# Router logits from un-normed sums beside the output projection of a two-block transformer on one Trainium2 core

## The reference

```python
x = x + gate1 * (merged @ w_out)
h2 = rmsnorm(x, norm2_w) * (1.0 + scale2) + shift2
x = x + gate2 * hierarchical_moe(h2, ...)

def hierarchical_moe(h, w_rg, b_rg, w_re, b_re, w_gate, w_up, w_down):
    g_logits = hf @ w_rg + b_rg               # 4 groups, take the best
    e_logits = hf @ w_re + b_re               # 4 x 8 experts, take the best two of the group
    ...
    for e in range(32):
        act = silu(hf @ w_gate[e]) * (hf @ w_up[e])
        y = y + combine[:, e:e + 1] * (act @ w_down[e])
```

## Time and profile before

| | us |
|---|---|
| median of 3 runs (1857.8 to 1860.01) | 1859.15 |
| the profiled execution | 1859.66 |
| its span, first to last instruction | 1857.8 |
| mean granted TensorE clock | 0.938 |

### The profile page before, as it was taken

One profiled execution on the slowest core, in us unless ns is written; L12 is line 12 of the kernel. 1 busy time (PEld: TensorE's weight loads), 2 busy tenths in 40 slices (PEclk: granted clock), 3 DMA queues, 4 the chain that ended last, 5 costly groups with the idle time before them and its releaser, 6 DMA issues.

```text
span 1857.8 us, 20218 instructions
## 1 busy us (share of the span) xinstructions
PE 1670.6 (90%) x8343; PEld 1247.3 (67%) x8343; DVE 804.0 (43%) x1325; ACT 541.0 (29%) x852; POOL 54.7 (3%) x75
## 2 busy tenths in 40 slices
PE   4999999999887998989899799999999896987883
PEld 3986777777676787878788577688678775433331
DVE  5545343354353666556212684436662535111113
ACT  5334354344322322212112432331353212111111
POOL 3000000000000000000000000000000000111110
PEclk8998999999998899999999799999999987998987
DMA  4322222122223455464222122211213543999994
GB/s 126 125 91 46 68 69 68 62 71 73 68 69 110 133 165 182 159 202 136 91 91 85 46 68 69 68 56 58 69 46 138 197 167 132 387 418 420 419 390 164
DMA packets 146256, 260.33 MB, mean 140 GB/s; under 512 B 16036, under 2 KB 120640, under 8 KB 132464
## 3 DMA queue, kind: packets, MB, share of 16 engines
q1 hardware_dynamic: 140240, 249.82, 38.0%
q0 software_dynamic: 5920, 9.16, 1.4%
HBM read 253.71 MB, written 14.68 MB: 144 GB/s over the span
## 4 chain that ended last, share of the span: by engine, by line
PE 44%; DVE 4%; issue 2%; DMA 1%; ACT 1%; POOLq 0%; DVEq 0%; ACTq 0%
PE psum L2206 8%; PE psum L2207 8%; PE psum L2208 8%; PE psum L2768 7%; PE psum L2785 3%; PE psum L2746 1%; PE psum L2395 1%; PE psum L2597 1%; DVE WL L1413 0%; PE psum L2415 0%; PE psum L2343 0%; PE psum L2353 0%; PE psum L2352 0%; DMA Xg<-h_rows,tok 0%; PE psum L2374 0%
## 5 line engine op out<-in xcount | busy, mean ns | idle before, releaser
L2206 PE MATMUL psum<-AH,WH 128*128 128x512 f32 (+1 forms) x1240 | 497.9, 402 | 46.5 <-DVE WL L1413 15.0
L2207 PE MATMUL psum<-AL,WH 128*128 128x512 f32 (+1 forms) x1240 | 481.6, 388 | 0.0
L2208 PE MATMUL psum<-AH,WL 128*128 128x512 f32 (+1 forms) x1240 | 478.4, 386 | 0.0
L2206 PEld LDWEIGHTS psum<-AH,WH 128*128 128x128 f32 x1240 | 240.4, 194 | 110.8 <-DVE WL L1413 26.5
L1413 DVE TENSOR_TENSOR WL<-raw,WH 128x2048 fp32r<-128x2048 f32 (+1 forms) x100 | 226.6, 2267 | 201.0 <-ACT WH L913 201.0
L2208 PEld LDWEIGHTS psum<-AH,WL 128*128 128x128 f32 x1240 | 240.5, 194 | 48.0
L2207 PEld LDWEIGHTS psum<-AL,WH 128*128 128x128 f32 x1240 | 240.9, 194 | 45.7 <-issue 3.1
L913 ACT ACTIVATE WH<-raw 128x2048 fp32r<-128x2048 f32 (+1 forms) x100 | 189.0, 1890 | 196.0 <-PE psum L2208 129.3
L2768 PE MATMUL psum<-WE,XT 128*64 128x512 f32 x544 | 133.3, 646 | 25.4 <-issue 24.5
L2768 PEld LDWEIGHTS psum<-WE,XT 128*64 128x64 f32 x544 | 48.4, 149 | 108.7 <-issue 108.7
L1820 DVE SCALAR_TENSOR_TENSOR cst<-araw,pcol,cst 128x256 f32<-128x256 f32 x168 | 81.6, 486 | 6.0
(11 more groups left out here) (481 smaller groups left out, 1896.3 us busy)
## 6 DMA issues: line engine op xcount, KB each, us to landing
raw<-w_in SPq DMA_DIRECT2D x45, 1024.0 KB, 5.2
WE<-w_gate SPq DMA_DIRECT2D x34, 1024.0 KB, 20.8
WE<-w_up SPq DMA_DIRECT2D x34, 1024.0 KB, 29.0
WE<-w_down SPq DMA_DIRECT2D x34, 1024.0 KB, 28.6
araw<-w_ada SPq DMA_DIRECT2D x24, 1024.0 KB, 5.2
raw<-w_ffn_in SPq DMA_DIRECT2D x22, 1024.0 KB, 5.2
raw<-w_ffn_out SPq DMA_DIRECT2D x11, 1024.0 KB, 4.9
raw<-w_out SPq DMA_DIRECT2D x8, 1024.0 KB, 5.1
```

The source lines that it names most:

```text
L2206: MM(dst, lh, rh, start=first, stop=False)
L2207: MM(dst, lh, rl, start=False, stop=False)
L2208: return MM(dst, ll, rh, start=False, stop=last)
```

## The change

The logits are taken from the raw `hT`. With gain = (1 + scale2) * norm2_w, the normed token is rms * x * gain + shift2, so its logit is rms * (x @ (gain * wr)) + (shift2 @ wr + bias). Accordingly:

- `router_shift` (PE, 8 products of 36 columns) and `router_scale` (DVE) put shift2 @ wr into `rb` and scale `wr` by gain. PE does this right after group 0 of `wo2`, where it now waits for `wr`.
- `rows_of(c)` is run by PE for each chunk c, seven times between dense products and once behind the last: 4 sums of squares, 4 logit products (tokens on the partitions, 36 columns) and 4 transposes of `hT`. ACT copies each set of transposes to `xtm`.
- Behind the last slab the spread of the norm, `H2`, its 32 transposes, `lgT` and the later transposes of `hT` are gone. DVE multiplies the logits by rms and adds `rb`.
- `h2t` is now `xtm` times rms, 1024 columns by ACT from SBUF, in a ring of two rows of tokens; POOL stores it, not SP, and its gather waits for all four stores.
- gain and shift2 are applied at the experts' copies `XT`: four instructions of 128 columns on ACT and four on DVE for a tile, where one of 512 stood on each. Their columns in the experts' order come by a small round trip through DRAM (`gs_dram`), started at `km` 0.
- `ranks` makes 5 products (128, 128, 96, 64 and 32 columns) where 14 stood.
- The constants of the routing (`routing_numbers`) are computed by DVE at the start of `wo2`.
- The second half of tile 1 moves to a slot over `AH`, and is loaded after the last dense product; so are both halves of tile 2.

```diff
 (SP, expert loads)
                 if s["name"] == ("wo2", 2):
                     sp.wait_ge(*when("m2_lo", KC))
                     load_expert(sp, 0, 1, NE // 2)
+                if s["name"] == ("wo2", 3):
                     load_expert(sp, 1, 0, 1)
-                if s["name"] == ("wo2", 3):
-                    load_expert(sp, 1, 1, NE // 2 + 1)
...
             sp.wait_ge(*when("dense_ready", len(GROUPS)))
+            load_expert(sp, 1, 1, NE // 2 + 1)
             load_expert(sp, 2, 0, 2)
-
-            for t in range(NB):
-                sp.wait_ge(*when("h2t_copied", 2 * t + 2))
-                sp.dma_start(h2_dram[P * t:P * t + P, :], h2t[:, t, :]).then_inc(S_("h2_stored"), 16)
-            sp.wait_ge(*when("spots_used", 1))
+            sp.wait_ge(*when("n_two_summed", KC))
+            load_expert(sp, 2, 1, NE // 2 + 2)
             sp.wait_ge(*when("overflow_ready", 1))
-            load_expert(sp, 2, 1, NE // 2 + 2)
 (POOL)
-            pool.wait_ge(*when("h2_stored", 16 * NB))
+            for t in range(NB):
+                pool.wait_ge(*when("h2t_copied", t + 1))
+                pool.dma_start(h2_dram[P * t:P * t + P, :], h2t[:, t % 2, :]).then_inc(S_(f"h2_stored{t % 2}"), 16)
+            for n in range(2):
+                pool.wait_ge(*when(f"h2_stored{n}", 16 * len(range(n, NB, 2))))
             pool.wait_ge(*when("tokens_ready", 1))
 (ACT)
+            def rows_copy(c):
+                act.wait_ge(*when("x_major", c + 1))
+                nc.scalar.activation(xtm[:, :, P * c:P * c + P], bank(6 + c % 2).rearrange("p (t n) -> p t n", t=NB), ACT.Copy
+                                     ).then_inc(S_("xtm_copied"), 1)
...
-                nc.scalar.activation(XT[:, t % 2, 0:512], bank(0), ACT.Copy).then_inc(S_("xt_even"), 1)
+                for k in range(4):
+                    nc.scalar.activation(XT[:, t % 2, P * k:P * k + P], bank(0, P, P * k), ACT.Identity, scale=gain8[:, k:k + 1],
+                                         bias=shift8[:, k:k + 1]).then_inc(S_("xt_even"), 1)
 (DVE)
+            def router_scale():
+                dve.wait_ge(*when("router_shift", 1))
+                link(V.tensor_tensor(rb, bank(7, NG + NE), rb, ALU.add))
+                dve.wait_ge(*when("router_landed", 32))
+                V.tensor_tensor(wr, wr, gain.unsqueeze(2).to_broadcast([P, KC, NG + NE]), ALU.mult).then_inc(S_("router_scaled"), 1)
...
-            norm_apply("n_two", hT, gain, False, out_name="h2_ready", shift=shift2, dst=H2)
...
-            dve.wait_ge(*when("logits_ready", 1))
+            dve.wait_ge(*when("router_mm", 1))
             link(V.tensor_tensor(lg, bank(5, NB * (NG + NE)).rearrange("p (t n) -> p t n", t=NB),
-                                 rb.unsqueeze(1).to_broadcast([P, NB, NG + NE]), ALU.add))
+                                 stat[:, 48:52].unsqueeze(2).to_broadcast([P, NB, NG + NE]), ALU.mult))
+            link(V.tensor_tensor(lg, lg, rb.unsqueeze(1).to_broadcast([P, NB, NG + NE]), ALU.add))
 (PE)
+            def router_shift():
+                pe.wait_ge(*when("router_landed", 32))
+                for c in range(KC):
+                    ins = MM(bank(7, NG + NE), shift2[:, c:c + 1].to_broadcast([P, P]), wr[:, c, :], start=c == 0, stop=c == KC - 1)
+                ins.then_inc(S_("router_shift"), 1)
+
+            def rows_of(c):
+                if c == 0:
+                    pe.wait_ge(*when("router_scaled", 1))
+                pe.wait_ge(*when("n_two_squared", c + 1))
+                for t in range(NB):
+                    ins = MM(bank(4, 1, t), sq2[:, c % 4, P * t:P * t + P], ones[:, 0:1], start=c == t == 0, stop=c == KC - 1,
+                             skip_group_check=True)
+                ins.then_inc(S_("n_two_summed"), 1)
+                for t in range(NB):
+                    ins = MM(bank(5, NG + NE, (NG + NE) * t), hT[:, c, P * t:P * t + P], wr[:, c, :], start=c == t == 0,
+                             stop=c == KC - 1, skip_group_check=True)
+                if c == KC - 1:
+                    ins.then_inc(S_("router_mm"), 1)
+                if c >= 2:
+                    pe.wait_ge(*when("xtm_copied", c - 1))
+                for t in range(NB):
+                    ins = nc.tensor.transpose(bank(6 + c % 2, P, P * t), hT[:, c, P * t:P * t + P], ident)
+                ins.then_inc(S_("x_major"), 1)
...
-                for t in range(NB):
-                    for b in range(t + 1):
-                        MM(bank(7, NE, NE * t), K("strict") if b == t else ones, both[:, b, :], start=b == 0, stop=b == t)
-                for b in range(NB):
-                    ins = MM(bank(7, NE, NE * NB), ones, both[:, b, :], start=b == 0, stop=b == NB - 1)
+                MM(bank(7, NB * NE), K("strict"), both.rearrange("p t n -> p (t n)"), start=True, stop=False, skip_group_check=True)
+                for b in range(1, NB + 1):
+                    n = NE * (NB + 1 - b)
+                    ins = MM(bank(7, n, NE * b), ones, both.rearrange("p t n -> p (t n)")[:, 0:n], start=False, stop=b == NB,
+                             skip_group_check=True)
...
-                    for _ in pieces(s):
-                        pass
+                    for j, _ in enumerate(pieces(s)):
+                        if s["name"][0] == "wo2":
+                            i = s["name"][1]
+                            if (i, j) == (0, 1):
+                                router_shift()
+                            if (i, j) == (1, 0):
+                                rows_of(0)
+                            if i and j == 1:
+                                rows_of(2 * i - 1)
+                            if i and j == 2:
+                                rows_of(2 * i)
                     end(s)
-            norm_pe("n_two")
+            rows_of(KC - 1)
```

More of the change, by code:

```diff
@@ L1825, in _, with routing_numbers @@
             summed = []
+            def routing_numbers():
+                link(V.tensor_scalar(later, K("expert"), -1000.0, None, ALU.add))
+                link(V.tensor_tensor_scan(iota, ones, ones, -1.0, ALU.mult, ALU.add))
+                link(V.tensor_scalar(thr[:, 0, :], iota[:, 1:8], float(CAP), 0.5, ALU.mult, ALU.add))
+                link(V.tensor_scalar(thr[:, 1, :], thr[:, 0, :], -1.0, None, ALU.add))
+                link(V.tensor_scalar(places[:, 0, :], K("expert"), NE // 2 - 0.5, float(CAP), ALU.is_ge, ALU.mult))
+                link(V.scalar_tensor_tensor(places[:, 1, :], places[:, 0, :], -0.5 * NE / CAP, K("expert"), ALU.mult, ALU.add))
+                for c in range(2):
+                    V.tensor_scalar(ids[:, NB * c:NB * c + NB, 0], K("token"), 1.0, None, ALU.add).then_inc(S_("dve_chain"), 1)
+                    V.tensor_scalar(ids[:, NB * c:NB * c + NB, 1], K("token"), 2.0, c + 1.0, ALU.mult, ALU.add).then_inc(S_("dve_chain"), 1)
+                    chain.n += 2
+            def router_scale():
[3 more added lines that the diff above has]
+                V.tensor_tensor(wr, wr, gain.unsqueeze(2).to_broadcast([P, KC, NG + NE]), ALU.mult).then_inc(S_("router_scaled"), 1)
             def modulation():
@@ L2158, in xt_copy @@
                 dve.wait_ge(*when("tx_done", t + 1))
-                V.tensor_copy(XT[:, t % 2, 512:], bank(1)).then_inc(S_("xt_odd"), 1)
+                for k in range(4, KC):
+                    V.tensor_scalar(XT[:, t % 2, P * k:P * k + P], bank(1, P, P * (k - 4)), gain8[:, k:k + 1], shift8[:, k:k + 1],
+                                    ALU.mult, ALU.add).then_inc(S_("xt_odd"), 1)
             def gated(t):
@@ L2329, in ml_guard @@
             def ml_guard(h):
[L2330 to L2331 removed]
+                pe.wait_ge(*(when("ml_h", h) if h else when("gs_rows", 1)))
                 sel = ident[0:4, h:h + 1].to_broadcast([4, P])
@@ L2618, in end @@
                     columns_of_pending()
-                if k in ("wo", "wo2") and name[1]:
-                    norm_sums("n_ffn" if k == "wo" else "n_two", 2 * name[1] - 2, 2 * name[1])
+                if k == "wo" and name[1]:
+                    norm_sums(2 * name[1] - 2, 2 * name[1])
                 if name == ("qm", 0):
                     gates_rows()
+                if name == ("km", 0):
+                    pe.wait_ge(*when("gain_two", 1))
+                    for n, x in enumerate((gain, shift2)):
+                        ins = nc.tensor.transpose(bank(7, P, P * n)[0:KC], x, ident)
+                    ins.then_inc(S_("gs_turned"), 1)
                 if name == ("qm", 1):
```

184 lines of the change are left out of this document (84 added, 100 removed).

## The result

| | us |
|---|---|
| before, median of 4 runs (1857.8 to 1860.01) | 1859.24 |
| after, median of 4 runs (1876.13 to 1877.57) | 1877.14 |
| after, span of the profiled execution | 1874.3 |

The changed kernel is slower: the ratio is 1.0096, with a 95% interval of 1.0083 to 1.0108. The forecast was 1863.2 with a range up to 1872.0, so the direction was right, the time lies 13.9 us above the forecast and 5.1 us outside the range.

The account below looks back on a forecast made before the run. Experts are bound by weight loads, so the end follows tile 0's gate_up, behind a PE-bound dense stretch and a chain. Dense stretch +23.9 us, chain -19.9, total +4.0: forecast 1863.2 us, range 1855.5 to 1872.

Parts of the forecast that it names:

- (a): Dense wo2 stretch: seven rows_of calls of 2.29 us each, less two blocks of sums removed; net +12.4 us.
- (b): Dense wo2 stretch: the eight products of router_shift add 1.7 us.
- (e): At km 0: two transposes and their copy for the small DRAM round trip add 0.3 us.
- (c): Behind group 0 of wo2: PE stands waiting for wr, +5.4 us; lower bound 2.5.
- (d): Behind the wait for wr: PE's clock falls to half, slowing small and dense products, +4.1 us; lower bound 1.7.
- first rival: wr lands before PE asks, so (c) and (d) vanish: -9.5 us, 1853.7 us, faster; chance 0.12.
- (f): Chain behind the last group's addition: logits lg done 4.8 us after it instead of 19.3, gain 14.5 us.
- (g): Chain from logits through ranks: unchanged up to both, then five rank products in 2.7 us; gain 3.0 us.
- (i): Before the gather: four token-row stores delay its issue to 28.9 us after the last group; loss 1.4, bounds 0 and 4.
- (k): Tile 0's XT copy: four operations instead of one add 0.3 us; in later tiles the loads cover the delay.
- The third: Rival: the clock falls inside the rows_of calls, 2.35 us each, seven costing 16: 1879 us; chance 0.15.
- The fourth: Rival: stores land late and the gather runs beside a load, +3 to +5 us: 1866 to 1869 us; chance 0.13.

Follow-up runs that it names:

- e5: Kernel before with only the XT copies split into four instructions of 128 columns each on ACT and DVE: 1860.12 us, ratio 1.001.
- e2: e1 with the router_shift products and router_scale moved behind group 1 of wo2 instead of group 0: 1855.13 us, ratio 0.9977.
- e1: Changed kernel with router_mm given its own counter, out of the shared one ahead of x_major: 1864.45 us, ratio 1.002.
- e3: Kernel before with only the 14 rank products replaced by the change's five: 1855.58 us, ratio 0.9979.
- e4: e2 with four buffers for token rows instead of two, so no row waits for a store: 1852.63 us, ratio 0.9965.
- e6: e4 with the load of tile 2's second half (3 MB) held until ACT has written the fourth token row: 1851.87 us, ratio 0.9965.
- e8: e6 with both halves of tile 2 (6 MB) held until the fourth token row is written: 1854.07 us, ratio 0.9965.
- e7: e2 with the transposes of the seven rows_of calls between dense products made five times over: 1866.04 us, ratio 1.0044.
- e2b: Changed kernel with only the later place of router_shift and router_scale, router_mm still in the shared count: 1870.0 us, ratio 1.006.
- e9: e6 with the four token-row stores issued by SP, ahead of tile 2's second half, instead of POOL: 1853.17 us, ratio 0.9963.

## Why the prediction was right and wrong

**What bounds the kernel.** Right. The end lies 276.6 to 277.4 us behind L in every kernel of the table, and what the later tiles pay for `XT` is covered (e5 leaves at most 3.5 us for all seventeen).

**(a), (b), (e).** (a) and (b) are right: 13.6 measured in e2, 14.1 forecast. A call is 0.79 + 0.92 + 0.48 = 2.2 us. The 0.3 of (e) lies ahead of W, where the executions spread by 7.7 us, and no run shows it.

**(c), (d).** Right: `wr` took 7.84 us, PE stood for 4.95, the clock was 0.50 for `router_shift` and the next 5.6 us; taking both away moved W to E by 9.6 (9.5 forecast). So the first rival is refuted for this transfer. One reading beside it was wrong. The 5.2 us of the earlier trace rows, taken for a small transfer with quiet engines and set against the 2.0 us fixed of the Trainium skill (DMA: Bandwidth & Descriptors, section "Anatomy of one DMA"), was issued at 11.37, and the DMA share was 1.09 from 11 to 14 and 1.13 from 14 to 17. The changed kernel has truly quiet ones: four of 4 KB from POOL, issued from 1100.88 to 1103.8 at a DMA share of 0.02 to 0.04, landed in 1.6 to 1.9 us. That agrees with the fixed part; the estimate of 2.3 us fails for `wr` beside a load of 3 MB, and the lower bound of (c) rested on a transfer under full engines.

**ACT's queue, the step that failed.** The prediction priced ACT's copies at nothing: "ACT's copies of the transposes fit into its idle time, 4.9 us before each square". As work they do; what it left out is which event each copy waits for and what is queued behind it. Its last paragraph named a gap ahead of `rows_of` that waits for ACT's copy as a cost left out. That cost came, by a longer way: not PE's transposes wait for the copy, but the next slab's weights do, and through them the square. e1 prices it: 12.7 us of the 13.9 by which the forecast missed in the medians, 10.9 of 12.7 in the two lengths. All of it could have been read from the order of events in `pe_steps` in the change, against the place where PE raises `router_mm`; the diff in front of the prediction doesn't show that list, and the prediction never looked at a wait's target.

**(f).** Right where the copies are on time: `lg` is done at E + 4.5 in e1 and E + 5.1 in e2 (4.8 forecast). In the changed kernel it is E + 6.7, by the copy in front of the root. Of these 2 us only one reaches the gather (e1), for it waits for the stores.

**(g), (h).** Ranks: 2.5 us in after and e1, 2.7 forecast. In e3 they took 1.8, with a clock of 0.68 in the 3 us around them (0.50 in after), and in e2, e4, e6 and e8 1.7, which the forecast had not allowed for. Token numbers at E + 26.1 in e1, 26.6 forecast.

**(i).** The mechanism was right and the size short: the gather went out at E + 30.3 in e1 and E + 31.3 in after, 28.9 forecast, 31.5 the bound. This 2.4 is the larger part of what E to L missed.

**(j), (k).** The gather took 3.97 us (4.3 forecast). `XT` cost 0.8 instead of 0.3, for ACT's four operations of 128 columns take 1.50 us, 0.38 each. Tile 0's `gate_up` took 9.46 us where 9.04 stood, a term that the sum held at nothing.

**The rivals.** The third had the nearest time, 1879, for a wrong reason: in the `wo2` slabs the clock fell only behind stands, and seven calls made longer (e7) didn't move it. That a burst without a stand can lose the clock was true all the same (the one at 1402.66), but not of these calls. The fourth happened in part, as stores that landed late; the gather itself was quick.

**The change as meant** is faster than before: e2, with the two misplacements mended, gives 0.9977, and with four buffers 0.9965. The five rank products alone give 0.9979. What remains open is whether the logits in token-major form, without the ranks, gain anything beyond the measurement: e2 against e3 is 1855.13 against 1855.58. Nor was the new order of the expert loads tried by itself.

## What to carry to other kernels

Where many events share one counter, read the list against the order in which the engine raises them: a wait for an event asks for everything listed ahead of it, and one that is raised later shifts all the waits behind it. An engine whose work fits into its idle time is free only if its waits end on time; follow what is queued behind each, here slab weights, and who waits for that. Price a small DMA by a transfer under the same load, and look at the DMA share of its stretch before calling it quiet. A stand of PE cost here its length and between half of it and all of it again in clock, so a small move that takes one away was worth up to twice what its row says.

## What the runs showed of the hardware

- Calls of 3.9 us of transposes, one-column and 36-column products between dense ones, seven times over, stayed at a granted clock of 1.00 (e7), while a 4.4 us burst of one-column products alone, with no stand ahead of it, ended at 0.50 (before, at 1402.66). Standing for 3.3 us between full stretches was followed by 0.50, for some 3.5 us (after) to some 7 us (e2b).
- The price of such a fall differs between equal stands: 1.8 us each in the changed kernel, 3.2 us each in e2b.
- A store of 512 KB took 3.4 to 3.9 us with little in flight (e8), 8 to 12 in the changed kernel, 15.3 in e4. The Trainium skill, DMA: Bandwidth & Descriptors, section "Anatomy of one DMA", gives an estimate of 3.2 us (2.0 fixed and the bytes at 436 GB/s). e8's first three lie 0.2 to 0.7 above it; the others show what loads in flight add.
- Two loads (6 MB) issued at the same time as a store, on another queue, delayed it (10.0 us against 3.4 for the one before it, e8). With a load issued behind it on the same queue the last store landed 3.9 us sooner behind E than with that load on another queue (e9 against e6).
- Four POOL transfers of 4 KB landed in 1.6 to 1.9 us with quiet DMA engines (after, at 1100.88); one of 16 KB took 5.2 us while the engines were full (before, at 11.37), and 128 KB took 7.8 to 8.1 beside a 3 MB load.
